# Loading the down matrices of experts 8 to 31 from ScalarE's queue instead of SyncE's

## The chip, the cores and the metric

The kernel runs on one core of a Trainium2 chip. The metric is the device time of one launch in microseconds. The kernel before takes 1076.98 us, the median of 3 runs (1076.45 to 1077.9). Everything below is read from one profiled execution of the program on that core.

## The reference

The program computes two transformer layers on 256 tokens of width 1024, in float32. The change touches only the last part, the mixture of experts of the second layer: 32 experts with three matrices each (gate `w1`, up `w3`, down `w2`). Reduced to what matters:

```
h     = x + attention branches ...                  # dense layer, second mixer: not touched
n     = rms_norm(h, g_ffn_2)                        # 256 x 1024
gates = two experts out of 32 for every token
for e in range(32):
    hid[e] = silu(n_e @ w1[e]) * (n_e @ w3[e])      # w1, w3: 1024 x 512
    y[e]   = hid[e] @ w2[e]                         # w2: 512 x 1024
out   = rms_norm(h + sum_e gate[e] * y[e], g_final)   # (residual and gain as in the reference)
```

All 32 experts are computed, each for the 32 token slots that it can take in a pass. Each of the 96 matrices has 524288 float32 values, so 2048 KB, and is read from HBM once.

## The kernel before

**Stages.** The first part of the program (dense layer, mixer of the second layer) ends near 640 us. From there on the experts run, in eight groups of four (`QUAD`). For each group TensorE first gathers the tokens of four experts (L1272). For each expert it then does 64 gate matmuls and 64 up matmuls (L1328), adds the result of the expert before to the tokens (L1312), and does the down matmuls (L1344). At the first expert of a group it also spreads the gate weights (L1296). In the trace's names the matrices are `arena`, `even_w`, `third_w` or `extra_w`, all `<-in_w`.

**Who does what for one expert.** TensorE's gate and up results stand in PSUM. ScalarE applies silu (L1651), VectorE multiplies by the up result (L2274) and transposes it (L2279), TensorE does the down matmuls, ScalarE copies their result `y_part` (L1656), and TensorE adds it to the tokens. After expert 31 ScalarE squares the sums (L1668), and the final norm and the output follow.

**Places of the weights.** From expert 8 on, even experts use the three places `even_w`, odd ones `odd_w`. A matrix of expert e may be loaded when TensorE has used the same matrix of expert e - 2. Experts 0 to 7 use some further places and are loaded by a written list of `expert_load` calls.

**The queue.** All weights are issued by SyncE (SP), in order of use: gate, up, down of one expert, then of the next. `stream` (L756 to L766) is the loop for experts 8 to 31; ahead of each transfer SP waits for a count: `e_w1` counts finished gate matmul groups, `e_up` up groups, `e_y` down groups. The semaphore `landed_w` of a place rises by 16 when a transfer has landed, and TensorE waits for it. ScalarE's queue carries only small loads at the very start (L1370 to L1375), and GpSimd's one late load, a gain row (L787).

**More than one pass.** If an expert has more than 32 tokens, all experts run again (`n_pass`, read from `passes_i`). With these inputs there is one pass.

Of the kernel before, what the change touches and what calls it, by code (L numbers as in the profile page):

```python
# [48 lines left out]
EXPERTS = GROUPS * PER_GROUP  # L49
# [3 lines left out]
QUAD = 4  # L53
# [236 lines left out]
def layers_kernel(nc, a, table, windows, out):  # L290
# [187 lines left out]
    for m, (u, _, _) in enumerate(piece_list):  # L478
        piece_at.setdefault(u, m)
# [6 lines left out]
    def slots(first, blocks):  # L486

        return arena[:, first:first + 2, :].rearrange("p s (c n) -> p (s c) n", c=blocks // 2)

    even_w, odd_w = ([even_w3[:, :, :] if s is None else slots(s, b) for s, b in zip(at3, (KC, KC, 4))]  # L490
                     for at3 in SLOT_OF)
# [4 lines left out]
    def sem(name):  # L496
        return nc.alloc_semaphore(name)
# [45 lines left out]
    landed_w = [[sem(f"{parity}_w{n}") for n in (1, 3, 2)] for parity in ("even", "odd")]  # L543
# [104 lines left out]
    def _(sp):  # L648
# [43 lines left out]
        def expert_load(e, places, which, landing):  # L692
            src = sources[which][:, bass.ds(e, 1), :, :].rearrange("p e c n -> p (e c) n")
            sp.dma_start(places[which], src).then_inc(landing, 16)
# [63 lines left out]
        def stream(pass_, lo_pair):  # L758

            with sp.Fori(lo_pair, EXPERTS // 2) as i:  # L760
                for odd in range(2):
                    e = sp.snap(i * 2 + odd)
                    used = sp.snap(i * 2 + (pass_ * EXPERTS + odd - 1))
                    for which in range(3):
                        sp.wait_ge((e_w1, e_up, e_y)[which], used)
                        expert_load(e, (even_w, odd_w)[odd], which, landed_w[odd][which])  # L766

        stream(0, 4)
        sp.wait_ge(passes_ready, 1)
        n_pass = sp.value_load(passes_i[0:1, 0:1], min_val=1, max_val=T // SLOTS)  # L770
        with sp.If(n_pass > 1):
            with sp.Fori(1, n_pass) as again:
                stream(again, 0)
            sp.nop()
# [75 lines left out]
    def _(pe):  # L850
# [262 lines left out]
        def values(pair, lo):  # L1113

            k = pair[1]
            pe.wait_ge(right_ready, k + 1)
            if k >= lo + 4:
                pe.wait_ge(pair_out, k // 2 - 1)
            both = [(head_in(x), ps[DH * (x % 2):DH * (x % 2) + DH, (7, 3)[x // 2 % 2], :], right_b[x % 2])
                    for x in pair]  # L1120
            for (_, _, v, _), o, r in both:
                mm(o[:, 0:T], v[:, 0, :], r[:, 0:T], start=True, stop=False)  # L1122
            for (_, _, v, _), o, r in both:
                if kind(k) == "x":
                    last = mm(o[:, 0:T], v[:, 1, :], r[:, T:2 * T], start=False, stop=True)
                else:
                    last = mm(o[:, P:T], v[:, 1, :], r[:, T:CAUSAL], start=False, stop=True)
                last.then_inc(o_done, 1)
# [230 lines left out]
    def _(act):  # L1359
# [146 lines left out]
        for step, *arg in plan:  # L1506
# [17 lines left out]
            elif step == "residual":  # L1524
                n = arg[0] + 2
# [116 lines left out]
        fn(exp_out[:, :, :].rearrange("p a b -> p (a b)"), exp_in[:, :, :].rearrange("p a b -> p (a b)"), ACT.Exp)\  # L1642
            .then_inc(route_exp, 1)

        def quad_body(q):
            e0 = act.snap(q * QUAD) if not isinstance(q, int) else 0
            act.wait_ge(xg_half, q + 1)
            fn(xg[:, 0:4, :].rearrange("p a b -> p (a b)"), ps[:, 4, :], ACT.Copy).then_inc(xg_part, 1)
            for e in range(QUAD):
                act.wait_ge(e_up, e0 + (e + 1))  # L1650
                fn(silu_e[:, :], ps[:, 6, 0:P], ACT.Silu).then_inc(e_silu, 1)  # L1651
                if e == 0:
                    act.wait_ge(gt_done, q + 1)
                    fn(gate_T[:, 0:2, :].rearrange("p a b -> p (a b)"), ps[:, 4, :], ACT.Copy).then_inc(gt_ready, 1)
                act.wait_ge(e_y, e0 + (e + 1))
                fn(y_part[:, e % 2, :], ps[:, 7, 0:UC], ACT.Copy).then_inc(e_yA, 1)  # L1656

        quad_body(0)
        act.wait_ge(passes_ready, 1)
        n_pass = act.value_load(passes_i[0:1, 0:1], min_val=1, max_val=T // SLOTS)  # L1660
        with act.Fori(1, n_pass * (EXPERTS // QUAD)) as q:
            quad_body(q)
        act.wait_ge(comb_done, n_pass * EXPERTS)
        for i in range(2):
            if i:
# [673 lines left out]
```

## Time and profile before

| | |
|---|---|
| median of 3 runs | 1076.98 us |
| the profiled execution | 1077.02 us, with a span of 1074.8 us |
| TensorE (PE) busy | 925.6 us, 86% of the span |
| VectorE (DVE) busy | 502.5 us, 47% |
| ScalarE (ACT) busy | 365.5 us, 34% |
| SyncE's DMA queue (q1) | 304.72 MB |
| ScalarE's DMA queue (q10) | 0.28 MB |
| granted TensorE clock, mean | 0.953 of full speed |

The time of a run is a little longer than the span, which goes from the first to the last instruction of the trace. Busy shares are means over stages that differ: they say little about the last 430 us by themselves. A DMA share of 1.00 means that all 16 DMA engines were busy throughout that stretch; the records overlap slightly, so a share may read a little over 1. TensorE's clock has two levels here, 2.4 GHz (1.00) and 1.2 GHz (0.50).

### The profile page before, as it was taken

The numbers are of one execution on the slowest core, as the hardware profiler recorded it, in microseconds if no ns is written. First come the engines' busy times: TensorE is split into PE (matmuls) and PEld (weight loads), VectorE is DVE, ScalarE is ACT, GpSimd is POOL, SyncE is SP. The second block draws the span as 40 slices with busy tenths as digits, with TensorE's granted clock in tenths as the row PEclk, the third lists the DMA queues.
The fourth block names the chain that finished last, engine by engine and source line by source line (L and its number), as shares of the span: only waits on it lengthen the run. The fifth ranks groups of instructions, "written<-read, shape, count | busy, mean of one in ns | idle before, by whom it ended". The sixth has DMA issues, their size and how long they took to land.

```text
span 1074.8 us, 22602 instructions
## 1 busy us (share of the span) xinstructions
PE 925.6 (86%) x9976; PEld 763.6 (71%) x9976; DVE 502.5 (47%) x806; ACT 365.5 (34%) x518; POOL 30.5 (3%) x34
## 2 busy tenths in 40 slices
PE   9999999999999999999999988786657667676764
PEld 8998877888888888989777876664545445454542
DVE  4746768687676667889877651110000100010101
ACT  6445765454444345444666330010000000000001
POOL 0200002110000001000000000000000000000000
PEclk9999999999999999999999999998998978898987
DMA  9954434545655644544457999999999999999994
GB/s 330 309 181 163 154 131 155 181 153 196 195 188 166 215 154 157 158 157 157 157 186 285 391 420 424 425 426 425 427 429 429 429 427 427 428 427 429 429 428 186
DMA packets 86285, 309.99 MB, mean 288 GB/s; under 512 B 5580, under 2 KB 46232, under 8 KB 73432
## 3 DMA queue, kind: packets, MB, share of 16 engines
q1 hardware_dynamic: 84560, 304.72, 73.5%
q0 software_dynamic: 1056, 4.20, 1.2%
q8 instruction: 42, 0.69, 0.3%
q10 hardware_dynamic: 616, 0.28, 0.1%
q14 instruction: 11, 0.09, 0.0%
HBM read 308.15 MB, written 1.05 MB: 288 GB/s over the span
## 4 chain that ended last, share of the span: by engine, by line
PE 58%; issue 38%; DVE 1%; ACT 1%; DMA 1%; POOL 0%; SPq 0%; POOLq 0%; DVEq 0%; ACTq 0%
PE ps L855 13%; PE ps L857 12%; PE ps L856 12%; PE ps L974 8%; PE ps L976 4%; PE ps L1328 1%; PE ps L1122 1%; PE ps L1110 1%; DMA arena<-in_w_in 1%; PE ps L1344 1%; PE ps L1272 0%; PE ps L949 0%; PE ps L1084 0%; DVE h L1784 0%; PE ps L1083 0%
## 5 line engine op out<-in xcount | busy, mean ns | idle before, releaser
L1328 PE MATMUL ps<-arena,xg 128*32 128x128 f32 x2816 | 110.4, 322 | 75.3 <-DMA arena<-in_w 71.2
L1697 DVE TENSOR_TENSOR w_split<-arena,w_split 128x2048 fp32r<-128x2048 f32 x70 | 159.3, 2287 | 30.1 <-ACT w_split L1391 29.6
L1328 PEld LDWEIGHTS ps<-arena,xg 128*32 128x32 f32 x2816 | 94.4, 130 | 93.8 <-DMA arena<-in_w 85.2
L2274 DVE TENSOR_TENSOR hid<-silu_e,ps 128x128 f32<-128x128 f32 x32 | 12.1, 378 | 315.8 <-ACT silu_e L1651 315.8
L1391 ACT ACTIVATE w_split<-arena 128x2048 fp32r<-128x2048 f32 x70 | 132.8, 1900 | 66.2 <-PE ps L857 57.8
L974 PE MATMUL ps<-x_both,w_split 128*128 128x512 f32 x352 | 124.6, 398 | 0.8 <-DVE x_both L1792 0.8
L855 PE MATMUL ps<-w_split,x_both 128*128 128x512 f32 x256 | 101.9, 398 | 0.9 <-DVE w_split L1748 0.9
L856 PE MATMUL ps<-w_split,x_both 128*128 128x512 f32 x256 | 99.8, 390 | 0.0
L857 PE MATMUL ps<-w_split,x_both 128*128 128x512 f32 x256 | 99.8, 390 | 0.0
L976 PE MATMUL ps<-x_both,w_split 128*128 128x256 f32 x352 | 98.8, 281 | 0.0
L1651 ACT ACTIVATE silu_e<-ps 128x128 f32<-128x128 f32 x32 | 8.9, 277 | 245.2 <-PE ps L1328 245.2
L1344 PE MATMUL ps<-arena,hid_T 128*32 128x256 f32 x960 | 64.5, 409 | 27.7 <-DMA arena<-in_w 27.0
L974 PEld LDWEIGHTS ps<-x_both,w_split 128*128 128x128 f32 x352 | 66.1, 188 | 17.0 <-issue 1.0
L855 PE MATMUL ps<-x_both,w_split 128*128 128x256 f32 (+1 forms) x256 | 73.0, 285 | 0.8 <-DVE x_both L1792 0.8
L857 PE MATMUL ps<-x_both,w_split 128*128 128x256 f32 (+1 forms) x256 | 72.3, 283 | 0.0
L856 PE MATMUL ps<-x_both,w_split 128*128 128x256 f32 (+1 forms) x256 | 72.3, 283 | 0.0
L1344 PEld LDWEIGHTS ps<-arena,hid_T 128*32 128x32 f32 x960 | 31.6, 115 | 55.0 <-issue 32.7
L855 PE MATMUL ps<-w_split,o_hi 128*128 128x512 f32 (+1 forms) x176 | 68.2, 387 | 0.5 <-DVE gates L1911 0.5
L1707 DVE TENSOR_TENSOR w_split<-arena,w_split 128x2048 fp32r<-128x2048 f32 x24 | 55.0, 2293 | 26.3 <-ACT w_split L1401 25.3
L857 PE MATMUL ps<-w_split,o_lo 128*128 128x512 f32 (+1 forms) x176 | 67.1, 381 | 0.0
L856 PE MATMUL ps<-w_split,o_hi 128*128 128x512 f32 (+1 forms) x176 | 67.0, 380 | 0.0
L976 PEld LDWEIGHTS ps<-x_both,w_split 128*128 128x128 f32 x352 | 66.5, 189 | 0.4
(318 smaller groups left out, 1460.0 us busy)
## 6 DMA issues: line engine op xcount, KB each, us to landing
arena<-in_w SPq DMA_DIRECT2D x71, 2048.0 KB, 26.1
arena<-in_w_in SPq DMA_DIRECT2D x41, 1024.0 KB, 5.2
even_w<-in_w SPq DMA_DIRECT2D x13, 2048.0 KB, 27.3
arena<-in_w_ffn_in SPq DMA_DIRECT2D x22, 1024.0 KB, 5.0
third_w<-in_w SPq DMA_DIRECT2D x6, 2048.0 KB, 15.8
arena<-in_w_ffn_out SPq DMA_DIRECT2D x11, 1024.0 KB, 4.9
arena<-in_w_out SPq DMA_DIRECT2D x8, 1024.0 KB, 6.8
arena<-in_w SPq DMA_DIRECT2D x6, 1024.0 KB, 7.1
```

Source lines behind the costliest of these rows:

```text
L855: mm(dst, l_hi, r_hi, start=start, stop=False)
L856: mm(dst, l_hi, r_lo, start=False, stop=False)
L857: return mm(dst, l_lo, r_hi, start=False, stop=stop)
L974: mm(ps[:, bank + n, :], hi[:, c, col], x_both[:, c, :, :].rearrange("p a b -> p (a b)"), start=c == 0, stop=False)
L976: last = mm(ps[:, bank + n, 0:T], lo[:, c, col], x_hi[:, c, :], start=False, stop=c == kc - 1)
L1110: last = nc.tensor.transpose(m[:, P * t:P * t + P], src[:, P * t:P * t + P], ident)
L1328: last = mm(ps[SLOTS * g:SLOTS * g + SLOTS, 6, P * n:P * n + P], xg[:, c, SLOTS * e:SLOTS * e + SLOTS], places[n][:, c, P * g:P * g + P], ...
L1344: last = mm(ps[SLOTS * g:SLOTS * g + SLOTS, 7, 0:UC], hid_T[:, SLOTS * b:SLOTS * b + SLOTS], places[2][:, b, UC * g:UC * g + UC], start=b ...
L1391: fn(w_hi[:, u % 3, 0:n], ring[:, u % 3, 0:n], ACT.Copy).then_inc(hi_ready, 1)
L1697: v.tensor_tensor(w_lo[:, u % 3, 0:n], ring[:, u % 3, 0:n], w_hi[:, u % 3, 0:n].bitcast(F32), ALU.subtract).then_inc(lo_ready, 1)
L1707: v.tensor_tensor(w_lo[:, s, :], ring[:, s, :], w_hi[:, s, :].bitcast(F32), ALU.subtract)\
L2274: v.tensor_tensor(hid[:, :].rearrange("p (b i) -> p i b", b=4), silu_e[:, :].rearrange("p (i b) -> p i b", b=4), ps[:, 6, P:2 * P].rearran ...
```

## The change

SyncE's loop `stream` issues only the gate and up matrices of experts 8 to 31. Their down matrices are issued by ScalarE: right after it has copied the result of expert e (`y_part`), it issues the down matrix of expert e + 2, into the place that expert e has just used. Since ScalarE itself waits for `e_y` before the copy, it needs no further wait. ScalarE's loop over the groups is split for it: group 1 is written out (with loads after its experts 2 and 3), groups 2 to 6 are a loop (loads after each expert), group 7 is written out (loads after its first two experts), and the loop for further passes stands behind a condition, without loads. In further passes SyncE loads all three matrices, as before.

```diff
@@ SyncE, stream @@
-                    for which in range(3):
+                    for which in range(2 if isinstance(pass_, int) else 3):
                         sp.wait_ge((e_w1, e_up, e_y)[which], used)
                         expert_load(e, (even_w, odd_w)[odd], which, landed_w[odd][which])
@@ ScalarE @@
+        w2_rows = a["w2_2"][0].rearrange("e (p c) n -> p e c n", c=4)
+
-        def quad_body(q):
-            e0 = act.snap(q * QUAD) if not isinstance(q, int) else 0
+        def quad_body(q, load=()):
+            e0 = act.snap(q * QUAD) if not isinstance(q, int) else q * QUAD
...
                 fn(y_part[:, e % 2, :], ps[:, 7, 0:UC], ACT.Copy).then_inc(e_yA, 1)
+                if e in load:
+                    coming = act.snap(q * QUAD + (e + 2)) if not isinstance(q, int) else q * QUAD + e + 2
+                    act.dma_start((even_w, odd_w)[e % 2][2],
+                                  w2_rows[:, bass.ds(coming, 1), :, :].rearrange("p e c n -> p (e c) n"))\
+                        .then_inc(landed_w[e % 2][2], 16)
 
         quad_body(0)
         act.wait_ge(passes_ready, 1)
         n_pass = act.value_load(passes_i[0:1, 0:1], min_val=1, max_val=T // SLOTS)
-        with act.Fori(1, n_pass * (EXPERTS // QUAD)) as q:
-            quad_body(q)
+        quad_body(1, (2, 3))
+        with act.Fori(2, EXPERTS // QUAD - 1) as q:
+            quad_body(q, range(QUAD))
+        quad_body(EXPERTS // QUAD - 1, (0, 1))
+        with act.If(n_pass > 1):
+            with act.Fori(EXPERTS // QUAD, n_pass * (EXPERTS // QUAD)) as q:
+                quad_body(q)
+            act.nop()
```

On SyncE, in the loop over pairs of experts (L694 is the transfer; the first of a piece is gate, then up, then down), the order of instructions before and after differs like this:

```order
 L694 DMA arena<-in_w_2 128x4096
 L694 DMA even_w_122<-in_w_2 128x4096
-L694 DMA arena<-in_w_2 128x4096
 L694 ISA
-L694 DMA arena<-in_w_2 128x4096 x3
+L694 DMA arena<-in_w_2 128x4096 x2
 L760 REGISTER_ALU
 L760 COMPARE_AND_BRANCH
```

Both down transfers have left the loop: the one of the even expert (the third row) and the one of the odd expert (one of three).

On ScalarE, in its loop over groups before, one expert is a silu (L1651) and a copy of the result (L1656):

```order
L1651 ACTIVATE silu_e<-ps 128x128 [waits e_up]
L1656 ACTIVATE y_part<-ps 128x256 [waits e_y]
L1650 REGISTER_ALU
L1651 ACTIVATE silu_e<-ps 128x128 [waits e_up]
L1656 ACTIVATE y_part<-ps 128x256 [waits e_y]
```

After, the same place in the loop for groups 2 to 6 (silu is now L1653, the copy L1658):

```order
L1653 ACTIVATE silu_e<-ps 128x128 [waits e_up]
L1658 ACTIVATE y_part<-ps 128x256 [waits e_y]
L1661 ISA
L1661 DMA arena<-in_w_2 128x4096
L1653 ACTIVATE silu_e<-ps 128x128 [waits e_up]
L1658 ACTIVATE y_part<-ps 128x256 [waits e_y]
```

A transfer and the instruction that works out its address now stand between the copy and the silu of the next expert.

Also on ScalarE, at the end of the experts: between the last copy of a result and the first square there were, before, these rows:

```order
L1656 ACTIVATE y_part<-ps 128x256 [waits e_y]
L1661 ISA
L1661 COMPARE_AND_BRANCH
L1663 REGISTER_ALU
L1668 ACTIVATE y_quad,sq_part<-ps 128x512 [waits comb_done]
```

After, the condition stands there, and behind it the loop for further passes, which is jumped over:

```order
L1658 ACTIVATE y_part<-ps 128x256 [waits e_y]
L1672 COMPARE_AND_BRANCH
L1673 UNCONDITIONAL_BRANCH
L1673 ISA
L1650 ACTIVATE xg<-ps 128x512 [waits xg_half]
...
L1673 ISA
L1673 COMPARE_AND_BRANCH
L1672 UNCONDITIONAL_BRANCH
L1676 REGISTER_ALU
L1681 ACTIVATE y_quad,sq_part<-ps 128x512 [waits comb_done]
```

The jump ahead of the final squares is new; the rows in between aren't executed with one pass.

## Rows read from the trace of the kernel before

**Rows 1.** The page's 40 slices: busy tenths of PE, clock, DMA, rate.

```profile
PE   9999999999999999999999988786657667676764
PEclk9999999999999999999999999998998978898987
DMA  9954434545655644544457999999999999999994
GB/s 330 309 181 163 154 131 155 181 153 196 195 188 166 215 154 157 158 157 157 157 186 285 391 420 424 425 426 425 427 429 429 429 427 427 428 427 429 429 428 186
```

**Rows 2.** Windows: stretch, length, busy of PE, PEld, DVE, ACT, POOL, clock, DMA share, GB/s.

```profile
700.00:1058.00 358.00, 238.99 (x4920) 184.19 (x4919) 31.29 (x84) 23.39 (x61) 0.00 (x0) 0.87 1.00 426
640.00:655.00 15.00, 11.30 (x292) 8.69 (x288) 1.38 (x3) 1.64 (x4) 0.00 (x0) 1.00 1.02 430
666.00:678.00 12.00, 11.00 (x207) 8.78 (x203) 2.03 (x7) 0.98 (x2) 0.48 (x1) 1.00 1.00 415
```

**Rows 3.** Waits of PE, 600 to 1075 us: total us, times, longest.

```profile
PE ps L1328 <- DMA arena<-in_w: 71.2, 30, 2.9
PE ps L1344 <- DMA arena<-in_w: 27.0, 24, 3.2
PE ps L1328 <- DMA even_w<-in_w: 15.0, 10, 2.9
```

**Rows 4.** Timeline from expert 31's gate matmuls on: start, us, engine; idle before in brackets.

```profile
1051.84 2.42 PE L1328 MATMUL ps<-arena,xg 128*32 128x128 f32 x64 [2.89 <-DMA arena<-in_w]
...
1056.72 3.53 PE L1328 MATMUL ps<-arena,xg 128*32 128x128 f32 x64 [2.47 <-DMA arena<-in_w]
...
1061.05 0.31 DVE L2279 STREAM_TRANSPOSE hid_T<-hid 128x128 f32<-128x128 f32 x1
...
1061.64 1.93 PE L1344 MATMUL ps<-arena,hid_T 128*32 128x256 f32 x32 [0.31 <-DMA arena<-in_w]
1063.64 0.38 ACT L1656 ACTIVATE y_part<-ps 128x256 f32<-128x256 f32 x1 [3.04 <-PE ps L1344]
...
1065.29 0.60 ACT L1668 ACTIVATE y_quad<-ps 128x512 f32<-128x512 f32 x1 [1.27 <-PE ps L1312]
```

**Rows 5.** Windows at the end of the weight stream, same columns as Rows 2.

```profile
1054.00:1056.00 2.00, 0.25 (x8) 0.00 (x0) 0.00 (x0) 0.00 (x0) 0.00 (x0) 0.50 0.81 344
1060.00:1061.00 1.00, 1.00 (x24) 0.72 (x16) 0.36 (x1) 0.28 (x1) 0.00 (x0) 1.00 0.04 16
1061.00:1062.00 1.00, 0.69 (x16) 0.28 (x12) 0.33 (x2) 0.00 (x0) 0.00 (x0) 1.00 0.00 0
```

**Rows 6.** DMA issues of the page: size, median us from issue to landing.

```profile
even_w<-in_w SPq DMA_DIRECT2D x13, 2048.0 KB, 27.3
```

**Rows 7.** DMA queues, 8 to 10 us, then 670 to 672: packets, MB, share.

```profile
q1 hardware_dynamic: 307, 0.60, 80.4%
q10 hardware_dynamic: 307, 0.16, 27.5%
...
q1 hardware_dynamic: 43, 0.69, 81.1%
q0 software_dynamic: 43, 0.18, 22.7%
```

**Rows 8.** Timeline of PE at other experts, columns as in Rows 4.

```profile
696.45 2.17 PE L1328 MATMUL ps<-third_w,xg 128*32 128x128 f32 x72 [2.54 <-issue]
...
699.86 1.93 PE L1344 MATMUL ps<-third_w,hid_T 128*32 128x256 f32 x32 [0.17 <-DVE hid_T L2279]
...
1027.36 1.96 PE L1328 MATMUL ps<-arena,xg 128*32 128x128 f32 x64 [1.31 <-DMA arena<-in_w]
...
1032.34 3.35 PE L1344 MATMUL ps<-arena,hid_T 128*32 128x256 f32 x32 [1.95 <-DMA arena<-in_w]
```

**Rows 9.** ScalarE: DMA issues at the start, and its waits from 700 us on.

```profile
0.78 0.61 ACTq L1370 DMA_DIRECT2D rows<-in_norm_mix_pre  x1
...
ACT silu_e L1651 <- PE ps L1328: 212.6, 25, 11.0
```

**Rows 10.** SyncE's last issues of weights, columns as in Rows 4.

```profile
1014.68 0.33 SPq L694 DMA_DIRECT2D even_w<-in_w  x1
...
1019.64 16.42 SPq L694 DMA_DIRECT2D arena<-in_w  x4
```

## The prediction

> **What bounds the kernel now.** I read the page's slices first. From about 620 us on the DMA row stands at 9 and the rate at 420 to 429 GB/s, while PE falls from 9 to 6 or 7 tenths [rows 1]. A stage in which the transfers never rest and TensorE does is bound by the transfers. The window of the expert stage confirms it: from 700 to 1058 us a DMA share of 1.00 and 426 GB/s, with PE busy 239 of 358 us [rows 2]. The list of PE's waits says for what it waits: weights, 71.2 + 27.0 + 15.0 = 113.2 us in all, no single wait over 3.2 us [rows 3]. Gate groups start at 1051.84, up groups at 1056.72 [rows 4], so one matrix of 2048 KB lands every 4.9 us, and an expert takes 3 x 4.9 = 14.7 us.
>
> The second reading is how deep the queue is. From issue to landing a matrix takes 27.3 us [rows 6], that is 27.3 / 4.9 = 5.6 matrices. So SP keeps all six places full, and the queue is nowhere short.
>
> The third is the end. DMA share falls from 0.81 in 1054 to 1056 us to 0.04 in 1060 to 1061 and to nothing after [rows 5]: the 16 engines don't end together, and the last one delivers the end of the last matrix, down of expert 31, just before 1061.64. There PE starts the last down group, released by a transfer, with hid_T done at 1061.05 + 0.31 = 1061.36 [rows 4]. From that start to the end of the span are 1074.8 - 1061.64 = 13.2 us of copy, sums, norm and output. So: the time is the last weight's landing, plus what must be computed after it, plus 2.2 us between span and run (1077.02 - 1074.8). The profiled run's 1077.02 us is the median (1076.98) but for 0.04.
>
> **The change part by part.**
>
> *Bytes.* None is added or removed. 24 down matrices move to another queue; the 16 DMA engines are the same. I cost the stream at 0 as long as something is always queued. SP alone now has four places (gate and up of two experts); PE holds one of them for at most 3.5 us [rows 4], so two to three matrices, 10 to 15 us of work, stand in SP's queue. That is more than the spread between first and last engine, about 6 us (1055 to 1061, [rows 5]). The last byte lands where it did, near 1061.6.
>
> *Order of arrival.* Two queues served at once is what the change really brings. Where two queues had work together, they got equal numbers of packets: 307 of SP's and 307 of ScalarE's within 8 to 10 us, 43 and 43 of SP's and GpSimd's within 670 to 672 us [rows 7]. Weight packets of all three kinds have the same size (2048 KB in 128 rows, 16 KB; 0.69 MB in 43 packets). So I expect a down matrix to get every second packet while both queues hold work: it needs 2 x 4.9 = 9.8 us, during which SP's queue advances by one matrix, instead of standing behind five. Per expert 9.8 us are shared and 4.9 us belong to SP alone, 14.7 us as before. Down matrices then come early, gate and up matrices in turn are the last to land.
>
> At the end: the down matrix of expert 31 is issued when expert 29's result is copied. At that time gate and up of experts 30 and 31 have at least in part still to land, four matrices, some 4 x 4.9 = 19.6 us. At half the packets it has landed after 9.8 us. The last to land is the up matrix of expert 31, near the 1061.6 us at which its down matrix came before. What came before that landing and now comes behind it is the term of the sum:
>
> - the 64 up matmuls of expert 31. They took 3.53 us at this place [rows 4], with the clock at 0.50; the same group at full clock took 1.96 [rows 8];
> - from their end to the first down matmul (silu, multiply, transpose; the addition of expert 30 lies beside them). In the tail that was 1061.64 - (1056.72 + 3.53) = 1.39 us [rows 4]; where no weight was waited for, 699.86 - (696.45 + 2.17) = 1.24 us [rows 8].
>
> Low end 1.96 + 1.24 = 3.2 us. High end 3.53 + 1.39 = 4.9 us, and if the last down group too falls into the low clock (3.35 instead of 1.93 us, [rows 8, 4]) 6.3 us. I take the middle of the two up groups, 2.75, and 1.39: 4.1 us. The clock decides between the ends, and it may go either way: with its down matrix at hand, PE does expert 30's down group right behind its up group and idles less just before the end, but the window mean of 0.87 [rows 2] holds both levels.
>
> *ScalarE's issues.* 24 of them, 0.61 us at most for the dearest issue on that queue at the start [rows 9], each with an instruction for its address. Behind it on ScalarE waits the silu of the next expert, and PE's down group waits for that. ScalarE waited 212.6 us in 25 places for that silu's input, 8.5 us each [rows 9]. Price 0; without that cover it would be 24 x 0.61 = 15 us, but a cover of 8.5 us over 0.6 doesn't go. The issue itself comes behind a 0.38 us copy, so each transfer starts about half a microsecond later than SP would have started it, in a queue that has 10 us of slack. Price 0.
>
> *SP.* The loop loses two issues and the waits for `e_y`. SP sat in waits anyway: from 1019.64 its last four issues took 16.42 us, at 0.33 us for one [rows 10]. The next gate matrix was never held up by `e_y`, since PE does the down group of expert e - 1 before the gate group of e. Gain 0.
>
> *Jump at the end.* ScalarE's path from the last copy to the first square gets a jump over the code of further passes. In between it had 1.27 us of idle time [rows 4]. A jump could cost an idle stretch like the one of 2.54 us that PE shows with nothing to wait for [rows 8]; 2.54 - 1.27 = 1.3 us would then show. Lower bound 0. I take 0, since ScalarE's and PE's code differ in size. The Trainium skill, Runtime: NRT & Kernel Launch, Instruction fetch mechanics, says that a taken branch whose target is outside the fetched pages stalls for a fetch; the trace has no row that isolates a jump on ScalarE, so it supports this rival without pricing it.
>
> Sum: 1077.02 + 4.1 = 1081.1 us, the same from the median. The main case's own range is 1077.0 + 3.2 to 1077.0 + 6.3: 1080.2 to 1083.3.
>
> **The rivals.**
>
> *A, not slower: arrival stays in the order of issue.* If the DMA engines work through transfers as they were issued, whichever queue they came from, the down matrix of 31 is again the last. Then all stays: 1077.0 us. The point from which it decides: the transfer has some 26 us from its issue (1035.73, the last of SP's four, from 1019.64 + 16.42 less 0.33, [rows 10]) to 1061.6, and needs 4.9 us of service; with under 4.9 / 26 = 19% of the packets it ends last. For it: GpSimd's and ScalarE's shares were seen only with small transfers. Against it: two windows with different partners and sizes, and equal counts in both [rows 7].
>
> *B, much slower: two interleaved streams run slower.* While GpSimd's gain row came in, 666 to 678 us, the rate was 415 against 426 in the long window [rows 2], 2.6% less. If the mix costs that during two thirds of the 358 us, 239 x 0.026 = 6.2 us come on top: 1087.3 us. For it: that row. Against it: those packets were 4 KB, and small packets alone may explain it.
>
> *C, faster: two streams run faster.* The best window shows 430 [rows 2]; against 426 that is 0.9% of 239 us, 2.2 us, which gives 1078.9. To get below 1074.8 it would take 4.1 + 2.2 = 6.3 us, 2.6%, so about 437 GB/s, which no window shows. The Trainium skill, DMA: Bandwidth & Descriptors, Issuing engines are not separate DMA queues, speaks against it: the same 16 engines serve all issuers, and a second one saves only issue time. By that rule alone, without a look at the order of arrival, the time would be A's; the row on equal packet counts agrees with its word that they interleave.
>
> *D, the jump shows:* 1081.1 + 1.3 = 1082.4 us.
>
> **How the numbers follow.** Main case 66%, A 15%, B 6%, C 7% (half of it under 1079.2 and half under 1074.8), D 6%. A measurement of this kernel can tell about 0.2%, 2.2 us, from no change: 1074.8 to 1079.2. Faster: 4%. Within: A with 15% and 3% of C, with 2% for a main case in which half of the term is hidden: 20%. Slower: 76%. The range takes A in at the low end and the clock and the jump at the high end: 1076.3 to 1083.8; B and the fast half of C are left out.
>
> **What would show it.** In the profile after: each down matrix lands before the gate matrix of the same expert or soon after, in about 10 us from issue instead of 27; PE's waits at the down matmuls for a transfer go from 27 us to almost nothing, and those at the gate and up matmuls rise by as much; DMA share and rate from 700 to 1058 us are the same; the last wait for a transfer is at the up matmuls of expert 31, near 1061.6 us, and about 17 us instead of 13.2 follow. Landing times of the down matrices near 27 us would make A right. A rate other than 424 to 430 GB/s would make B or C right. A last landing well before or after 1061 us at the same rate would mean that I have the spread of the engines wrong.

## The result and the profile after

The changed kernel takes 1080.37 us (median of 13 runs, 1079.1 to 1081.93); the kernel before, beside it, 1077.44 us (13 runs, 1076.41 to 1078.99). The ratio is 1.0026 with a 95% interval of 1.0018 to 1.0033, so it is slower by 2.9 us, small but clear. The profiled execution took 1080.37 us, its span is 1078.2 us, 3.4 us more than before.

The slices of the page (the second half of each row is the part to compare with [rows 1]):

```profile
PE   9999999999999999999999988765866657675763
PEclk9999999999999999999999999998887888798887
DMA  9954434545565644445458999999999999999993
GB/s 331 307 182 165 153 131 151 186 147 195 194 195 170 218 140 155 157 157 168 155 186 296 405 417 422 428 424 427 426 429 428 429 428 429 429 430 429 428 429 127
```

The stream is as full and as fast as before. The long window answers to the first of [rows 2], with the same 426 GB/s:

```profile
700.00:1058.00 358.00, 236.96 (x4898) 184.90 (x4896) 31.34 (x85) 23.44 (x61) 0.00 (x0) 0.85 1.00 426
```

Only the queue differs. DMA queues in the stretch from 880 to 940 us, first of the kernel before, then of the changed one (packets, MB, share of 16 engines):

```profile
q1 hardware_dynamic: 1766, 25.74, 100.8%
```

```profile
q1 hardware_dynamic: 1184, 17.30, 67.7%
q10 hardware_dynamic: 576, 8.39, 32.9%
```

25.74 MB against 17.30 + 8.39 = 25.69 MB: one third of the same stream now comes through ScalarE's queue. PE's waits from 600 us on answer to [rows 3]:

```profile
PE ps L1328 <- DMA arena<-in_w: 73.1, 23, 6.0
PE ps L1328 <- DMA even_w<-in_w: 43.6, 10, 7.8
```

The row of L1344, the down matmuls, with 27.0 us has gone: down matrices are always there. The gate and up groups wait 116.7 us where they waited 86.2; in all PE waits 116.7 us for weights, before 113.2. The waiting has moved, not shrunk.

The end, in the timeline of the changed kernel (answers to [rows 4]; L1653 is silu, L1658 the copy, L1681 the first square):

```profile
1055.43 1.96 PE L1328 MATMUL ps<-arena,xg 128*32 128x128 f32 x64 [3.27 <-DMA arena<-in_w]
1060.30 3.60 PE L1328 MATMUL ps<-arena,xg 128*32 128x128 f32 x64 [2.91 <-DMA arena<-in_w]
1063.83 1.15 PE L1312 MATMUL ps<-y_part,gate_T 32*128 32x256 f32 x16
1063.95 0.28 ACT L1653 ACTIVATE silu_e<-ps 128x128 f32<-128x128 f32 x1 [11.33 <-PE ps L1328]
...
1065.04 1.93 PE L1344 MATMUL ps<-arena,hid_T 128*32 128x256 f32 x32
...
1068.69 0.60 ACT L1681 ACTIVATE y_quad<-ps 128x512 f32<-128x512 f32 x1 [1.26 <-PE ps L1312]
```

The last group that a transfer releases is now the up group of expert 31. Before, it was the down group, one stage further on. Behind it come 1078.2 - 1060.30 = 17.9 us, against 13.2 us. Of the 4.7 us between the two, 3.60 are the up group at half clock, and 1065.04 - 1063.90 = 1.14 the way through silu and transpose. The stream itself ended 1.3 us earlier in this execution (1060.30 against 1061.64), hence 3.4 and not 4.7.

### The profile page after: what moved, and what is told of

Read it like the earlier page. It is cut to its first block, busy times and chain, and to the rows that moved or that the text cites. A ratio compares the mean times of both kernels' runs of the same rounds, so it can differ in the third digit from the quotient of the medians.

```text
span 1078.2 us, 22592 instructions
## 1 busy us (share of the span) xinstructions
PE 926.4 (86%) x9976; PEld 765.8 (71%) x9976; DVE 502.9 (47%) x806; ACT 365.6 (34%) x518; POOL 30.6 (3%) x34
## 4 chain that ended last, share of the span: by engine, by line
PE 58%; issue 38%; DVE 1%; ACT 1%; DMA 1%; POOL 0%; SPq 0%; POOLq 0%; DVEq 0%; ACTq 0%
PE ps L855 13%; PE ps L857 12%; PE ps L856 12%; PE ps L974 8%; PE ps L976 4%; PE ps L1328 1%; PE ps L1122 1%; PE ps L1344 1%; PE ps L1110 1%; DMA arena<-in_w_in 1%; PE ps L1272 0%; PE ps L949 0%; PE ps L1084 0%; DVE h L1797 0%; PE ps L1083 0%
## 5 line engine op out<-in xcount | busy, mean ns | idle before, releaser
L1328 PE MATMUL ps<-arena,xg 128*32 128x128 f32 x2816 | 105.4, 312 | 77.2 <-DMA arena<-in_w 73.1
L2287 DVE TENSOR_TENSOR hid<-silu_e,ps 128x128 f32<-128x128 f32 x32 | 12.1, 378 | 328.2 <-ACT silu_e L1653 328.2
L1328 PEld LDWEIGHTS ps<-arena,xg 128*32 128x32 f32 x2816 | 90.4, 126 | 92.2 <-DMA arena<-in_w 82.4
L1653 ACT ACTIVATE silu_e<-ps 128x128 f32<-128x128 f32 x32 | 8.9, 278 | 275.0 <-PE ps L1328 275.0
L1328 PE MATMUL ps<-even_w,xg 128*32 128x128 f32 x896 | 38.8, 345 | 43.6 <-DMA even_w<-in_w 43.6
L1328 PEld LDWEIGHTS ps<-even_w,xg 128*32 128x32 f32 x896 | 32.8, 140 | 47.8 <-DMA even_w<-in_w 46.4
## 6 DMA issues: line engine op xcount, KB each, us to landing
arena<-in_w ACTq DMA_DIRECT2D x24, 2048.0 KB, 13.9
```

The costliest lines, as they stand in the source:

```text
L1328: last = mm(ps[SLOTS * g:SLOTS * g + SLOTS, 6, P * n:P * n + P], xg[:, c, SLOTS * e:SLOTS * e + SLOTS], places[n][:, c, P * g:P * g + P], ...
L2287: v.tensor_tensor(hid[:, :].rearrange("p (b i) -> p i b", b=4), silu_e[:, :].rearrange("p (i b) -> p i b", b=4), ps[:, 6, P:2 * P].rearran ...
```

## The experiments

Each was timed beside the kernel before; of halves31_act there is a single execution. The table takes two numbers from each profile: when the last group released by a weight starts, and how far the span's end is from there. Its times are medians; the ratio and its interval compare the runs of a kernel with those of the kernel before beside it, and aren't exactly the quotient of the two medians.

| kernel | last group released by a weight | starts, us | to the span's end, us | time, us | ratio, 95% interval |
|---|---|---|---|---|---|
| before | down 31 | 1061.64 | 13.2 | 1077.44 | |
| changed | up 31 | 1060.30 | 17.9 | 1080.37 | 1.0018 to 1.0033 |
| down31_sp | down 31 | 1060.54 | 13.2 | 1076.69 | 0.9987 to 1.0005 |
| only31_act | up 31 | 1063.28 | 16.3 | 1080.83 | 1.0019 to 1.0039 |
| gates_act | down 31 | 1062.04 | 13.2 | 1077.25 | 0.9981 to 0.9999 |
| loops_only | down 31 | 1062.08 | 13.2 | 1076.74 | 0.9983 to 1.0002 |
| gate31_last | gate 31 | 1063.79 | 20.6 | 1084.39 | 1.0036 to 1.0072 |
| changed, again | up 31 | 1062.46 | 16.3 | 1080.03 | 1.0013 to 1.0035 |

The first four experiments had the kernel before at 1077.89 us beside them; gate31_last, after_again, after_warm and before_warm had it at 1077.26, after_warm8 and before_halves at 1077.7.

**down31_sp: one of 24 transfers goes back to SyncE**

```diff
         stream(0, 4)
+        sp.wait_ge(e_y, EXPERTS - 2)
+        expert_load(EXPERTS - 1, odd_w, 2, landed_w[1][2])
...
-        quad_body(EXPERTS // QUAD - 1, (0, 1))
+        quad_body(EXPERTS // QUAD - 1, (0,))
```

> The changed kernel, but the down matrix of expert 31 is issued by SyncE, behind the up matrix of 31, as before; ScalarE still issues 23 of the 24, with its new loops and its jump at the end. Theory (order of arrival at the end): the last matrix to land is again down of 31, its up group lies ahead of that landing, so the kernel before's time, 1077.4 us, within 1 us; the last wait for a transfer is at the down matmuls. Rival (interleaving two queues slows or delays the stream, or ScalarE's issues and jump cost): 23/24 of that is still there, so about 1080.3 us.

Measured 1076.69 us, ratio 0.9996 (0.9987 to 1.0005): the whole loss is gone, with 23 down matrices still on ScalarE's queue. Its timeline of PE at the end shows the old order:

```profile
1055.60 1.95 PE L1330 MATMUL ps<-arena,xg 128*32 128x128 f32 x64 [1.54 <-DMA arena<-in_w]
1057.48 1.15 PE L1314 MATMUL ps<-y_part,gate_T 32*128 32x256 f32 x16
1060.54 1.93 PE L1346 MATMUL ps<-arena,hid_T 128*32 128x256 f32 x32 [1.91 <-DMA arena<-in_w]
```

The up group (L1330 here) ran and ended while the down matrix was still on its way; the wait is at the down group (L1346).

**only31_act: one transfer alone on ScalarE's queue**

```diff
+        for e in (EXPERTS - 2, EXPERTS - 1):
+            for which in range(3 if e == EXPERTS - 2 else 2):
+                sp.wait_ge((e_w1, e_up, e_y)[which], e - 1)
+                expert_load(e, (even_w, odd_w)[e % 2], which, landed_w[e % 2][which])
...
+        quad_body(EXPERTS // QUAD - 1, (1,))      # ScalarE: only down 31
```

> One transfer alone: SyncE issues all weights in the old order but the down matrix of expert 31, which ScalarE issues after expert 29's result. Theory (order at the end): the full cost comes from this one transfer, so the changed kernel's 1080.4 us (+3 us), with the up group of 31 behind the last landing. Rival (interleaving or issue cost, spread over 24 transfers): 1/24 of 3 us, so 1077.5 us.

Measured 1080.83 us, ratio 1.0029 (1.0019 to 1.0039). A single transfer, issued at the same count, brings the whole loss. Its PE timeline:

```profile
1063.28 1.96 PE L1332 MATMUL ps<-arena,xg 128*32 128x128 f32 x64 [1.53 <-DMA arena<-in_w]
1065.17 1.15 PE L1316 MATMUL ps<-y_part,gate_T 32*128 32x256 f32 x16
1066.40 1.93 PE L1348 MATMUL ps<-arena,hid_T 128*32 128x256 f32 x32
```

Here the up group (L1332) ran at full clock, 1.96 us, and the down group starts 3.1 us after that group's start, without a wait.

**gates_act: ScalarE carries the gate matrices in place of the down ones**

```diff
                 fn(silu_e[:, :], ps[:, 6, 0:P], ACT.Silu).then_inc(e_silu, 1)
+                if e in load:
+                    coming = ...
+                    act.dma_start((even_w, odd_w)[e % 2][0], w1_rows[:, bass.ds(coming, 1), :, :]...)\
+                        .then_inc(landed_w[e % 2][0], 16)
```

> ScalarE issues the gate matrices of experts 8 to 31 (after silu) in place of the down matrices; SyncE issues up and down. Same number of transfers on ScalarE, same share of interleaving, but down of 31 is again the last to land. Theory: 1077.4 us within 1 us. Rival (interleaving costs stream time): 1080.4 us. If gate matrices landing early let up and down land later against each other, the end is still a down group: 13.2 us behind the last landing.

Measured 1077.25 us, ratio 0.999 (0.9981 to 0.9999). As many transfers on the second queue, as much interleaving (q10 with 50.33 MB from 700 to 1058 us, 33.1% of the engines' time), and no loss, since down of 31 is the last to land again. If anything it is 0.1% faster; the interval all but touches 1, and I claim nothing from it.

**loops_only: ScalarE's new loops and jump, without its transfers**

```diff
-                    for which in range(2 if isinstance(pass_, int) else 3):
+                    for which in range(3):
...
-        quad_body(1, (2, 3))
+        quad_body(1)                  # likewise for groups 2 to 7
```

> The changed kernel's ScalarE loops (group 1 and 7 written out, condition and jump ahead of the final squares) but without its transfers; SyncE issues all weights as before. Theory: nothing, 1077.4 us within 1 us, and ScalarE's idle time ahead of the first square stays 1.27 us. Rival (the jump shows): up to 1.3 us more, 1078.7 us, with the idle time ahead of the square longer.

Measured 1076.74 us, ratio 0.9992 (0.9983 to 1.0002). ScalarE's idle time ahead of the first square is what it was, and its releaser is PE, so the jump hides:

```profile
1065.72 0.60 ACT L1681 ACTIVATE y_quad<-ps 128x512 f32<-128x512 f32 x1 [1.27 <-PE ps L1312]
```

**gate31_last: one group more behind the last landing**

```diff
+        for e, order in ((EXPERTS - 2, (0, 1)), (EXPERTS - 1, (1, 0))):
+            for which in order:
+                sp.wait_ge((e_w1, e_up, e_y)[which], e - 1)
+                expert_load(e, (even_w, odd_w)[e % 2], which, landed_w[e % 2][which])
```

> The changed kernel with one swap: for expert 31 SyncE issues the up matrix before the gate matrix. TensorE still needs gate first, so both groups now come behind the last landing. Theory (work behind the last landing sets the end): one group of 64 matmuls more behind it, 1.96 us at full clock to 3.6 at half, so 1082.4 to 1084.0 us against the kernel before's 1077.9. Rival (the loss is the stream's or the queue's, not the tail's): no change from the changed kernel, about 1080.8 us.

Measured 1084.39 us, the median of 6 runs, ratio 1.0054 (1.0036 to 1.0072). I had expected 4.5 to 6.1 us more than the kernel before. By the ratio it is 5.8 us more, inside that; by the difference of the medians (1084.39 against 1077.26) it is 7.1, a little above. The profiled execution is the slowest of the six, 1086.39 us, and its stream ended late:

```profile
1063.79 6.22 PE L1332 MATMUL ps<-arena,xg 128*32 128x128 f32 x128 [6.17 <-DMA arena<-in_w]
1069.94 1.15 PE L1316 MATMUL ps<-y_part,gate_T 32*128 32x256 f32 x16
1071.18 1.93 PE L1348 MATMUL ps<-arena,hid_T 128*32 128x256 f32 x32
```

128 matmuls of gate and up in one piece, 6.22 us, with the clock at both levels. Behind the last landing there are now 20.6 us, 7.4 more than the kernel before's 13.2. One group behind it costs some 3 us, two cost 6 to 7.

**after_again: the changed kernel once more**

> The changed kernel once more, for a second profile and to stand beside the three others on one chip: 1080.8 us. Its last weight group starts between 1060 and 1063.5 us, as the kernels so far did, and the end follows 16.3 us (full clock) to 17.9 us (half clock) later.

Measured 1080.03 us, ratio 1.0024 (1.0013 to 1.0035). The second profile of the same program shows the other clock level:

```profile
1062.46 1.95 PE L1328 MATMUL ps<-arena,xg 128*32 128x128 f32 x64 [2.86 <-DMA arena<-in_w]
1064.34 1.15 PE L1312 MATMUL ps<-y_part,gate_T 32*128 32x256 f32 x16
1065.56 1.93 PE L1344 MATMUL ps<-arena,hid_T 128*32 128x256 f32 x32
```

1065.56 - 1062.46 = 3.1 us for the term, against 4.7 us (1065.04 - 1060.30) in the first profile.

**after_warm, before_warm, after_warm8: an attempt on the clock that failed**

```diff
+                    if looped:
+                        for _ in range((10, 20)[n]):
+                            mm(ps[:, 6, P * n:P * n + P], ones, ones, start=True, stop=True)
                     pe.wait_ge(landing[n], arrived)
```

> The changed kernel with matmuls on constants, whose results are overwritten, ahead of each wait for a gate matrix (10) and an up matrix (20) from group 2 on, in time in which TensorE waits for weights. If the half clock makes up part of the cost: the last up group runs at full clock, 1.96 instead of 3.6 us, so about 1.6 us less than the changed kernel where that had half clock, 1079 to 1079.5 us in the median. If the clock is no part, 1080.8 us; if the added matmuls hold up the real ones, more than that.

> The kernel before with the same added matmuls. Its last up group lies ahead of the last landing, so a faster one hides: hid_T is ready 1.6 us earlier, but the down group waits for its matrix, 0.3 us less at most. 1077.4 to 1077.9 us, no change that can be measured.

> The changed kernel with 8 matmuls on constants (some 1 to 2 us) ahead of each wait for an up matrix from group 2 on; their results are overwritten. With fewer than in after_warm, TensorE's work per expert should stay under the 14.7 us of an expert's transfers, so the stream is not held up. If the half clock in the last up group is part of the cost: that group at 1.96 us, median 0.5 to 1.5 us under the changed kernel, about 1079.3. If not: 1080.4. If the added matmuls still hold up the stream: more.

(after_warm8 has 8 such calls, ahead of the up group alone. Here and in the texts above an added matmul is one call; the trace shows two matmuls for each, x16 and 2.05 us for the 8.) Measured: 1135.77, 1133.85 and 1088.43 us, ratios 1.0553, 1.0521 and 1.0106, all slower, before_warm too, for which no change had been expected. The additions held up the stream. In after_warm8 the rate of the long window is 419 in place of 426 GB/s, and PE's waits from 700 us on have a row, the second one here, that among the kernels of this document only the three with added matmuls have:

```profile
PE ps L1331 <- DMA arena<-in_w: 34.9, 12, 5.8
PE ps L1272 <- issue: 28.5, 5, 6.5
```

Five times, once per turn of PE's loop, PE stood 5.7 us in the mean ahead of the first matmul of the loop with nothing to wait for that the profile shows. The queue that loads instructions (q8) moved 52 packets, 0.85 MB, from 700 to 1058 us; in the kernel before it moved 9, 0.15 MB. So the comparison of medians says nothing on the clock. What the profile of after_warm8 does give is one more end at full clock, though with added matmuls ahead of it: last up group at 1068.66, 1.96 us, span 1085.0, so 16.3 us.

**before_halves: is there something to gain at this end?**

```diff
+                    for half, landing in enumerate((last_half, landed_w[1][2])):
+                        part = slice(2 * half, 2 * half + 2)
+                        sp.dma_start(odd_w[2][:, part, :], sources[2][:, e, part, :]).then_inc(landing, 16)
```

> The kernel before, with the down matrix of expert 31 in two transfers of half the size and TensorE starting on the first half when it is there (TensorE's group 7 written out for it). Theory: only the work behind the last landing counts, so at most half a down group, 1 us, goes from behind it: 1076.3 to 1077.3 us against 1077.3. Where the last up group runs at half clock, hid_T comes only 0.3 us before that landing and the gain is 0.3 us. Rival: no gain or a loss of up to 1 us from smaller packets (8 KB) or TensorE's jump.

Measured 1078.68 us beside 1077.7, ratio 1.001 (1.0 to 1.0019): no gain, and if anything a loss of up to 1 us or so, as the rival had it; no run separates its two causes, the smaller packets and PE's jump. In its profile the up group ran at half clock and the down group waited for its left operand, not for a half of the matrix:

```profile
1057.69 3.53 PE L1339 MATMUL ps<-arena,xg 128*32 128x128 f32 x64 [2.48 <-DMA arena<-in_w]
1061.15 1.15 PE L1323 MATMUL ps<-y_part,gate_T 32*128 32x256 f32 x16
1062.48 1.93 PE L1361 MATMUL ps<-arena,hid_T 128*32 128x256 f32 x32 [0.18 <-DVE hid_T L2301]
```

**halves31_act: how a transfer on the second queue is served** (one execution, 1081.44 us)

```diff
+                    for half, landing in enumerate((last_half, landed_w[1][2])):
+                        part = slice(2 * half, 2 * half + 2)
+                        act.dma_start(odd_w[2][:, part, :], w2_rows[:, EXPERTS - 1, part, :]).then_inc(landing, 16)
```

> As only31_act, but ScalarE issues the down matrix of expert 31 as two transfers of half the size, to see why a transfer on ScalarE's queue took 13.9 us to land and not 9.8. If it starts about 3 us late (SP's work already taken up by the engines) and then gets every second packet: the first half lands after about 3 + 5 + 1 = 9 us, the second after about 14. If its share is simply under a half from the start (one packet in 2.8): the first lands after 7 us, the second after 14. The end as in only31_act: the last landing is up of 31, and 16.3 us (full clock) or 17.9 us (half) follow.

The halves landed 12.1 and 19.4 us after their issue, neither of my two pairs: I had left out that half a matrix in 128 rows has packets of 8 KB, and service goes by packets. From 1040 to 1046 us each queue got 116 packets, but SyncE's queue moved 1.65 MB and ScalarE's 0.92. The second needs 19.4 - 12.1 = 7.3 us more. Per engine a half is 8 packets, and each alternates with one of 16 KB of SP's: at 4.9 / 8 = 0.61 us and 0.31 us that is 8 x 0.92 = 7.3 us. So the first took 7.3 us of service too, and 12.1 - 7.3 = 4.8 us stand before and behind it. The late start shows in the changed kernel's queues. Its last down matrix was issued at 1041.76. The stretches 1041.76 to 1045.26 us, 1045.26 to 1045.76, and 1046.76 to 1054.76 us:

```profile
1041.76 0.34 ACTq L1661 DMA_DIRECT2D arena<-in_w  x1
```

```profile
q1 hardware_dynamic: 100, 1.51, 101.1%
```

```profile
q10 hardware_dynamic: 14, 0.23, 107.5%
```

```profile
q1 hardware_dynamic: 116, 1.75, 51.5%
q10 hardware_dynamic: 112, 1.70, 50.0%
```

For 3.5 us not one packet of the new transfer, then one for one. In halves31_act too the first packets came 3.5 to 4.0 us after the issue (none of ScalarE's queue up to 1039.11, 13 within 1039.11 to 1039.61, issued at 1035.61). At the start of the program, where SyncE had issued only a moment before, ScalarE's first transfer, issued at 0.78, had packets between 1.53 and 1.78 us, so within 1.0 us. That the 3.5 us are spent behind what the first queue has in work fits both, but no run varied the depth of that queue. The end of halves31_act came out as expected: last up group at 1062.97 us, 1.96 us, and 16.4 us to the end of the span (1079.4).

## Why the prediction was right

*Bytes and stream: right.* 426 GB/s and a DMA share of 1.00, as before. The last group released by a weight started between 1060.3 and 1063.8 us in the eight profiles of the table, in both orders, around the 1061.6 of the prediction. This scatter of some 3 us is as large as the effect; two single profiles therefore don't size the loss, the medians do.

*Order of arrival: right, and it is the whole cause.* One transfer put on ScalarE's queue gives the full loss (only31_act), one taken back removes it (down31_sp), 24 others there cost nothing (gates_act). The 9.8 us from issue to landing were too low. It took 13.9 us:

```profile
arena<-in_w ACTq DMA_DIRECT2D x24, 2048.0 KB, 13.9
```

The 9.8 us of alternation are there; what I missed is the time before the first packet, 3.5 us for down of 31, and some 0.5 us more. "About half a microsecond later than SP would have started it" was wrong too: down of 31 was issued at 1041.76 in one profile of the changed kernel and at 1038.23 in the other, against 1035.73 by SP before, because the result of expert 29 itself came later; in the first of them gate of 30 had landed by 1041.50, so three matrices, not four, were still to come. It changed nothing: down of 31 landed 13.8 us after its issue, at 1055.6, 4.7 us ahead of the last landing (1060.30), and was wanted at 1065.0. The margin was half of what the prediction counted, 19.6 - 9.8 = 9.8 us.

*The size of the term: 4.1 us taken, 3.1 at full clock and 4.7 at half.* Both levels occur in profiles of the same program; of the six that end on an up group (the changed kernel twice, only31_act, halves31_act, after_warm8 and, with the gate group in front, gate31_last) four have it wholly at full clock (after_warm8 with added matmuls ahead of it). The middle that I chose gives them equal weight. That PE would idle less just before the end held in one of the two profiles of the changed kernel only: in the first it waited 3.27 us ahead of the gate group of 31 and 2.91 ahead of the up group, which ran at half clock; in the second (after_again) the gate group followed straight on expert 30's down group, PE waited 2.86 us ahead of the up group alone, and it ran at full clock. The kernel before had 2.89 and 2.47 us, and half clock. The median of 2.9 us lies at the full-clock end, 3.1. The 1.39 us for silu and transpose was read where the down group had still 0.31 us to wait for its matrix; without that it is 1.14 to 1.16 (both profiles of the changed kernel, only31_act).

*ScalarE's issues and SP: 0, right.* An issue took 0.34 us behind the copy, and 24 of them cost nothing in gates_act. The jump: 0, right (loops_only), rival D falls.

*The other rivals.* A (order of issue kept) falls by the packet counts (116 and 112 side by side), the missing L1344 row and 13.9 us in place of 27. B and C (the mix changes the rate) fall by 426 GB/s in both, and by gates_act. What the Trainium skill, DMA: Bandwidth & Descriptors, Issuing engines are not separate DMA queues, says, that the same 16 engines serve all issuers and interleave their transfers, agrees with the trace: 426 GB/s with one queue and with two. That the time was not therefore the same came from the order of arrival.

*Left open.* What makes the stream end up to 3 us earlier or later from one execution to the next, and what sets the clock of the last group. PE's waits alone don't settle it: in only31_act it waited ahead of both groups of 31 as well (1.95 and 1.53 us), and the up group ran at full clock. The attempt to hold the clock up failed for another reason.

## What to carry to other kernels

In a stage that is bound by transfers, ask for the last matrix to land and how much must be computed behind it; here a second queue didn't change how fast the bytes came, but it did change which of them came last. Issue the transfer with the least work behind it last, on the same queue as those that it must not overtake. And read such an effect from medians and from the distance between last landing and end, since one profile's end may shift by more than the effect.

## What the runs showed of the hardware

- A transfer issued on the second queue while the first was full got its first packet 3.5 to 4.0 us after its issue, and was then served packet for packet at both packet sizes seen: 112 to 116 with 16 KB on both, and 116 to 116 with 8 KB against 16 KB, which gave it about a third of the bytes (0.92 of 2.57 MB; 7.3 us for 1 MB).
- PE's loop over groups turned without a stall before (L1272 after 0.33 us, 2.3 us in 7), but with 8 more matmul calls per expert in its body it stood 5.7 us per turn (28.5 us in 5), and as long with 30 more (28.4 us in 5). The instruction queue (q8) moved 9 packets from 700 to 1058 us before, and 52 with the 8 calls. The Trainium skill, Runtime: NRT & Kernel Launch, Instruction fetch mechanics, says that a taken branch to code outside the fetched pages must fetch it first; the trace agrees in that the idle time has no releaser, stands at the loop's start and comes with more instruction packets, but no run here varied the length of the code alone.
